# Output projection inside the expert stage's program, with a fine-grained start of head 0, in a one-core decoder-layer kernel

## The reference

```python
merged = sigmoid(parts[14]) * branch_a + sigmoid(parts[15]) * branch_b
x = x + ga1 * _rmsnorm(merged @ w_out, g_post1)          # output projection
h2 = _rmsnorm(x, g_pre2) * (1 + sc2) + sh2
# _peer(h2): per token, 8 heads
q = (h2 @ wq).reshape(T, 8, 256)
v1, i1 = top_k(q[..., :128] @ k1.T, 16)
v2, i2 = top_k(q[..., 128:] @ k2.T, 16)
sc, pos = top_k(all 256 sums v1 + v2, 16)                # 16 experts of 16384
g = softmax(sc)
act = gelu(einsum('td,thkd->thk', h2, u[eidx]))
f = einsum('thk,thkd->td', g * act, v[eidx])
x = x + ga2 * _rmsnorm(f, g_post2)
```

## Time and profile before

| | us |
|---|---|
| median of 3 runs (2635.83 to 2647.21) | 2636.57 |
| the profiled execution | 2642.91 |
| its span in the trace | 2641.1 |
| PE busy | 2226.0 (84%) |
| DVE busy | 1233.0 (47%) |
| ACT busy | 698.1 (26%) |
| POOL busy | 730.0 (28%) |
| gathers of the expert stage, issues on POOL | 576 |
| value matmuls (L1718) busy | 1084.4 |
| POOL idle ahead of a gather, for the value matmuls | 761.4 |
| DVE idle ahead of a dot product, for a gather | 428.4 |

### The profile page before, as it was taken

How to read it: one execution, slowest core, us unless ns; L and a number is a source line. 1 busy time by engine, 2 the same in 40 slices (tenths; PEclk the granted TensorE clock), 3 DMA queues, 4 the chain that set the end, 5 groups by cost and what they waited for, 6 DMA issues and landing times.

```text
span 2641.1 us, 24928 instructions
## 1 busy us (share of the span) xinstructions
PE 2226.0 (84%) x8970; PEld 1258.3 (48%) x8970; DVE 1233.0 (47%) x3186; ACT 698.1 (26%) x2115; POOL 730.0 (28%) x694
## 2 busy tenths in 40 slices
PE   6999989997787999878888887979788777787786
PEld 2777447865575776344443443434344333333221
DVE  1000001225232011457767667676776776767764
ACT  2000012332120001223333333333333443333322
POOL 0000001110101000034444443535444444454441
PEclk8999989997676999989999998989899898898899
DMA  7566648978672125079999999999999999999997
GB/s 279 228 252 253 249 142 303 318 307 333 222 270 104 60 72 179 4 281 420 416 418 417 413 419 409 420 406 420 410 418 412 415 421 404 420 415 414 418 418 301
DMA packets 134914, 850.41 MB, mean 322 GB/s; under 512 B 15121, under 2 KB 32817, under 8 KB 52989
## 3 DMA queue, kind: packets, MB, share of 16 engines
q0 software_dynamic: 85760, 691.32, 64.5%
q1 hardware_dynamic: 47740, 154.95, 15.9%
q10 hardware_dynamic: 1290, 2.55, 0.3%
HBM read 836.43 MB, written 99.37 MB: 354 GB/s over the span
## 4 chain that ended last, share of the span: by engine, by line
DMA 18%; PE 18%; DVE 17%; issue 2%; ACT 2%; POOL 1%; ACTq 0%; POOLq 0%
DMA pr_ring<-in_uv,pr_idx 18%; PE ps L1718 17%; DVE pr_ring L1859 4%; POOL pr_ring L1670 1%; DVE pr_hot L1843 1%; DVE pr_hot L1839 1%; DVE pr_ind L1820 1%; DVE pr_ind L1817 1%; DVE pr_pick L1846 1%; PE ps L1684 1%; ACT pr_coef L1777 1%; DVE pr_val L1819 1%; DVE pr_rest L1818 1%; DVE pr_val L1816 1%; DVE pr_pos L1820 1%
## 5 line engine op out<-in xcount | busy, mean ns | idle before, releaser
L1718 PE MATMUL ps<-pr_ring,pr_diag 128*128 128x512 f32 (+1 forms) x2304 | 1084.4, 626 | 288.9 <-ACT pr_diag L1781 288.5
L1670 POOL DMA_INDIRECT pr_ring<-in_uv,pr_idx x576 | 658.3, 1143 | 1129.1 <-PE ps L1718 761.4
L1859 DVE CUSTOM_DVE_ANT_0 pr_ring<-pr_ring,h 128x1024 f32<-128x1024 f32 x576 | 691.5, 1225 | 435.3 <-DMA pr_ring<-in_uv,pr_idx 428.4
L1718 PEld LDWEIGHTS ps<-pr_ring,pr_diag 128*128 128x128 f32 (+1 forms) x2304 | 438.4, 195 | 896.0 <-issue 510.2
L1772 ACT ACTIVATE pr_gel<-pr_dots 128x2 f32<-128x2 f32 x288 | 58.3, 202 | 637.5 <-DVE pr_dots L1859 637.3
L1781 ACT ACTIVATE pr_diag<-ident,pr_coef 128x128 f32<-128x128 f32 x512 | 173.5, 386 | 0.0
L1777 ACT ACTIVATE pr_coef<-pr_gel,pr_wgt 128x1 f32<-128x1 f32 x576 | 138.6, 287 | 27.6 <-ACT pr_gel L1772 1.1
L1415 PE MATMUL ps<-trunk,mg_ring 128*128 128x288 f32 x512 | 129.2, 412 | 12.6 <-DMA mg_ring<-in_w_merge 12.6
L1684 PE MATMUL ps<-trunk,pr_wq 128*128 128x192 f32 (+1 forms) x512 | 132.1, 412 | 2.3 <-PEq L1480 1.3
L430 PE MATMUL ps<-trunk,ap_ring 128*128 128x288 f32 x384 | 126.3, 411 | 2.9 <-PEq L323 2.9
L431 PE MATMUL ps<-trunk,ap_ring 128*128 128x288 f32 x384 | 125.2, 408 | 0.0
(11 more groups left out here) (289 smaller groups left out, 2036.4 us busy)
## 6 DMA issues: line engine op xcount, KB each, us to landing
out_win_s<-in_cache POOLq DMA_DIRECT2D x64, 1020.0 KB, 7.9
sa_ring<-in_cache SPq DMA_DIRECT2D x24, 1024.0 KB, 7.7
late_ring<-in_w_ada SPq DMA_DIRECT2D x8, 2048.0 KB, 17.6
sa_ring<-in_kcacheB SPq DMA_DIRECT2D x16, 1024.0 KB, 7.6
out_win_s<-in_cache POOLq DMA_DIRECT2D x16, 1008.0 KB, 10.7
ap_ring<-in_w_attn_qk SPq DMA_DIRECT2D x6, 2048.0 KB, 11.4
mg_ring<-in_w_merge SPq DMA_DIRECT2D x16, 768.0 KB, 4.2
sa_ring<-in_kcacheA SPq DMA_DIRECT2D x8, 1280.0 KB, 5.9
```

Of the source, the lines that this page charges most:

```text
L1670: pool.indirect_dma_start(ring[:, n % RING, :], None, d["uv"], bass.IndirectOffsetOnAxis(ap=idx[:, b % 4, j:j + 1], axis=0)).then_inc(arri ...
L1718: mm = pe.matmul(ps[0:r, bank + half, :], diag[:, n % RING, 0:r], ring[:, n % RING, o:o + CHUNK], start=h == 0 and j == 0, stop=b == FINAL ...
L1859: ins = dve.tensor_tensor_reduce(u, u, e.h2[:, BLOCKS[b][0], :], 1.0, 0.0, ALU.mult, ALU.add, dots[:, n % RING:n % RING + 1])
```

## The change

- **One program for the output projection and the experts** (`output_and_experts`). The gather ring (10 slots) is allocated first; w_out, `merged` and the sample tile's modulation rows lie in its slots 2 to 9, the prompt's rows where gate2 and fy come later. ACT's squares write into `h2` instead of a scratch tile. mg_ring moves into `h2`, which has room for AHEAD = 3 units.
- **Head 0's queries** come in six pieces instead of four: tile 0 (128 columns) twice, tiles 1 and 2 (256) twice, tiles 3 and 4 (192) twice. The first four have PSUM banks of their own.
- **Order.** PE: product(0), product(1), turn(0), product(2), two query pieces, turn(1), scores(0), product(3), turn(2), product(4), turn(3), two pieces, turn(4), scores(1), two pieces, the loop. DVE: tiles 0 to 2, route(0), tiles 3 and 4, the loop. ACT in the order of its list in the diff.
- **Gathers.** The first two follow route(0); the third waits for all products (`s_mm`), the ninth for all of h2 (`s_h2`), the eleventh as before for the first row's matmuls.
- **route(1)** stands after the third batch (FIRST_ROUTE = 3).
- **Constants.** c_tri, c_stri and mh_norm_g are loaded in conv_and_gates, ahead of the cache pieces, on a semaphore of their own; mLSTM's DVE no longer waits for C0 and n0 at its first chunk.

```diff
@@ conv_and_gates, SP
+                for dst, src in ((m.tri[:], "c_tri"), (m.stri[:], "c_stri"), (m.mhg[:], "mh_norm_g")):
+                    sp.dma_start(dst, d[src]).then_inc(m.s_const, 16)
                 sa.load(sp, range(sa.SR))
@@ mlstm, SP and DVE
-                sp.dma_start(tri[:], d["c_tri"]).then_inc(s_in, 16)
-                sp.dma_start(stri[:], d["c_stri"]).then_inc(s_in, 16)
-                sp.dma_start(mhg[:], d["mh_norm_g"]).then_inc(s_in, 16)
                 sp.dma_start(C0[:], d["C0"]).then_inc(s_in, 16)
                 sp.dma_start(n0[:], d["n0"]).then_inc(s_in, 16)
...
                 sa.normalised(dve, chain)
-                dve.wait_ge(s_in, 80)
+                dve.wait_ge(m.s_const, 48)
                 for c in range(NCH):
@@ merge
-    AHEAD, UNITS = 4, 2 * KD
+    AHEAD, UNITS = 3, 2 * KD
-        ring = sb("mg_ring", [P, AHEAD, KD + H, P])
+        unit = (KD + H) * P
+        ring = e.h2[:].rearrange("p t n -> p (t n)")[:, 0:AHEAD * unit].rearrange("p (a c n) -> p a c n", a=AHEAD, n=P)
@@ head 0's pieces
+HEAD0 = 6
+def query_count(h, piece):
+    return piece if h == 0 else HEAD0 + 4 * (h - 1) + piece
+def query_span(h, piece):
+    spans = ((0, P), (P, GROUPED), (GROUPED, T)) if h == 0 else ((0, GROUPED), (GROUPED, T))
+    return slice(*spans[piece // 2]), piece % 2
+def query_bank(h, piece):
+    return (4, 5, 2, 3)[piece] if h == 0 and piece < 4 else QUERY_BANK
-ROUTE, SCORE, SCORED = 6, 2, 4
+FIRST_ROUTE, ROUTE, SCORE, SCORED = 3, 6, 2, 4
@@ output_and_experts, SP
                 sp.dma_start(keysT[:], d["keysT"]).then_inc(s_keys, 16)
+                sp.wait_ge(s_h2, NCH)
                 sp.dma_start(e.h2[TS:P, PT, :], e.h2[0:TS, PT, :]).then_inc(s_in, 16)
...
                 for h in range(QUERY_SLOTS, PH):
-                    sp.wait_ge(s_q, 4 * (h - QUERY_SLOTS + 1))
+                    sp.wait_ge(s_q, query_count(h - QUERY_SLOTS + 1, 0))
@@ POOL
                         n = b * TOPK + j
+                        if n == 2:
+                            pool.wait_ge(s_mm, NCH)
+                        if n == 8:
+                            pool.wait_ge(s_h2, NCH)
                         if n >= RING:
                             pool.wait_ge(s_v, n - RING + 1)
@@ PE, ahead of the loop
+                product(0)
+                product(1)
+                turn(0)
+                product(2)
+                pe.wait_ge(s_tt, 1)
                 query(0, 0)
                 query(0, 1)
+                turn(1)
+                pe.wait_ge(s_y1, 3)
                 pe.wait_ge(s_keys, 16)
                 scores(0)
-                scores(1)
+                product(3)
+                turn(2)
+                product(PT)
+                turn(3)
+                pe.wait_ge(s_y1, 4)
+                pe.wait_ge(s_tt, 3)
                 query(0, 2)
                 query(0, 3)
+                turn(PT)
+                pe.wait_ge(s_y1, NCH)
+                scores(1)
+                pe.wait_ge(s_tt, NCH)
+                query(0, 4)
+                query(0, 5)
+                pe.wait_ge(s_qt, 4)
@@ ACT, ahead of the loop
+                product_root(0)
+                trunk_root(0)
+                turned(0)
+                product_root(1)
+                trunk_root(1)
+                product_root(2)
                 query_taken(0, 0)
                 query_taken(0, 1)
+                turned(1)
                 scores_taken(0)
-                scores_taken(1)
+                trunk_root(2)
+                route_exp(0)
+                turned(2)
+                product_root(3)
+                trunk_root(3)
+                product_root(PT)
+                turned(3)
                 query_taken(0, 2)
                 query_taken(0, 3)
-                route_exp(0)
+                trunk_root(PT)
+                turned(PT)
+                scores_taken(1)
+                query_taken(0, 4)
+                query_taken(0, 5)
@@ DVE
+                dve.wait_ge(front.s_x, 32)
+                dve.wait_ge(front.s_r, 16 * 3 * (1 + NS))
+                for i in range(GROUP):
+                    input_of(i)
                 route(0)
-                dve.wait_ge(s_in, 16 * (2 + NS))
+                for i in range(GROUP, NCH):
+                    input_of(i)
                 for b in range(len(BLOCKS)):
                     for q in range(PER):
-                        if b == 0 and q == 1:
+                        if b == 0 and q == FIRST_ROUTE:
                             route(1)
@@ build
-            output_projection(nc, k, d, e, o)
-        peer(nc, k, d, e)
+        e.ring, e.gf = sb("pr_ring", [P, RING, 2 * D]), sb("pr_gf", [P, 3, D])
+        o.w = flat[:, at:at + 2 * KD * CHUNK].rearrange("p (n c x) -> p n c x", n=2, c=KD)
...
+        merge(nc, k, d, e, o)
+        output_and_experts(nc, k, d, e, o)
```

More of the change, by code:

```diff
@@ L1584, with output_and_experts @@
 PER = TOPK // BATCH
-ROUTE, SCORE, SCORED = 6, 2, 4
+FIRST_ROUTE, ROUTE, SCORE, SCORED = 3, 6, 2, 4
 SQUARE, MEAN, ROOT, FINISH = 2, 3, 4, 5
-def peer(nc, k, d, e):
+def output_and_experts(nc, k, d, e, front):
     with ExitStack() as ctx:
         sb = lambda n, s, dt=F32: ctx.enter_context(nc.sbuf_tensor(n, s, dt))
-        ring = sb("pr_ring", [P, RING, 2 * D])
+        ring, gate2, fy = e.ring, e.gf[:, 0:2], e.gf[:, 2]
+        ss = sb("op_ss", [P, 2, NCH, 2])
+        ms = sb("op_ms", [P, 2, NCH])
+        rt = sb("op_rt", [P, 2, NCH])
+        rs = sb("op_rs", [P, 2, NCH])
+        s_mm, s_sq, s_ms, s_rt, s_y1, s_x1, s_h2, s_tr, s_tt = (
+            k.sem("op_" + n) for n in ("mm", "square", "ms", "root", "taken", "x1", "h2", "turned", "turned_taken"))
         keysT = sb("pr_keysT", [P, 2, NKEYS])
@@ L1676, in query @@
                 def query(h, piece):
-                    group, half = divmod(piece, 2)
-                    cols = slice(GROUPED, T) if group else slice(0, GROUPED)
+                    cols, half = query_span(h, piece)
                     if piece == 0:
                         pe.wait_ge(e.wq_ready[h % QUERY_SLOTS], 16 * (h // QUERY_SLOTS + 1))
-                    pe.wait_ge(s_qt, 4 * h + piece)
+                    if h > 0 or piece >= 4:
+                        pe.wait_ge(s_qt, query_count(h, piece))
                     for c in range(KD):
-                        mm = pe.matmul(ps[:, QUERY_BANK, 0:cols.stop - cols.start],
+                        mm = pe.matmul(ps[:, query_bank(h, piece), 0:cols.stop - cols.start],
                                        e.wq[:, h % QUERY_SLOTS, c, half * P:(half + 1) * P], e.h2T[:, c, cols],
@@ L1691, in scores @@
                     r = tile_rows(i)
-                    pe.wait_ge(s_qt, 4 * h + (2 if i < GROUP else 4))
+                    pe.wait_ge(s_qt, 2 if b == 0 else query_count(h, 4 if h == 0 else 2) if i < GROUP else query_count(h + 1, 0))
                     if b >= 1:
@@ L1731, in query_taken @@
                 def query_taken(h, piece):
-                    group, half = divmod(piece, 2)
-                    f = 2 * h + half
-                    act.wait_ge(s_q, 4 * h + piece + 1)
-                    if group == 0:
-                        ins = act.activation(first[:, f % 4, :], ps[:, QUERY_BANK, 0:GROUPED], ACT.Copy)
-                    else:
-                        ins = act.activation(e.later[:, f, :], ps[:, QUERY_BANK, 0:T - GROUPED], ACT.Copy)
-                    ins.then_inc(s_qt, 1)
+                    cols, half = query_span(h, piece)
+                    f, n = 2 * h + half, cols.stop - cols.start
+                    act.wait_ge(s_q, query_count(h, piece) + 1)
+                    dst = first[:, f % 4, cols] if cols.start < GROUPED else e.later[:, f, :]
+                    act.activation(dst, ps[:, query_bank(h, piece), 0:n], ACT.Copy).then_inc(s_qt, 1)
                 def scores_taken(b):
@@ L1782, in diags, with product_root @@
                                        scale=coef[:, o + j:o + j + 1]).then_inc(s_dg, 1)
+                def product_root(i):
+                    r = tile_rows(i)
+                    act.wait_ge(s_mm, i + 1)
+                    for n in range(2):
+                        chain.step(act.activation(e.h2[0:r, i, 0:CHUNK], ps[0:r, 2 * (i % 2) + n, :], ACT.Square,
+                                                  accum_out=ss[0:r, 0, i, n:n + 1]))
+                    act.sem_inc(s_sq, 1)
+                    act.wait_ge(s_ms, 2 * i + 1)
+                    act.activation(rt[0:r, 0, i:i + 1], ms[0:r, 0, i:i + 1], ACT.Sqrt).then_inc(s_rt, 1)
@@ new lines, in trunk_root, with turned @@
+                def trunk_root(i):
+                    r = tile_rows(i)
+                    act.wait_ge(s_x1, i + 1)
+                    act.activation(e.h2[0:r, i, :], e.x1[0:r, i, :], ACT.Square,
+                                   accum_out=ss[0:r, 1, i, 0:1]).then_inc(s_sq, 1)
+                    act.wait_ge(s_ms, 2 * i + 2)
```

(20 more changed lines are left out.)

167 lines of the change are left out of this document (59 added, 108 removed).

## The result

| | before | after |
|---|---|---|
| median of 4 runs each, us | 2641.89 (2635.83 to 2650.15) | 2612.12 (2593.49 to 2621.62) |
| the profiled execution | 2642.91 | 2621.62 |
| its span in the trace | 2641.1 | 2619.8 |

The ratio is 0.9869, with an interval of 0.9832 to 0.9906: 34.6 us faster (25 to 44), where 36.6 was forecast. The medians in the table lie 29.8 us apart; the ratio on record is not that of the medians, and its interval holds both. 2600 was under both medians and the range 2587 to 2614 holds the first.

What follows compares the result with a forecast made beforehand. The expert stage was taken as bound by a full DMA pipe of 576 gathers of 1 MB. Terms of 27.5 + 4.2 + 4.9 = 36.6 us off the median 2636.57 gave 2600 us, range 2587 to 2614.

Steps and rivals of the forecast that it cites:

- Term 1: Expert stage: ten rows fetched early and an earlier pipe restart, less a hole, save 27.5 us (22 to 32).
- all at full clock: Early bound for the first value matmul: 1136 us, with 128-column query pieces at 1.8 us, against 1139.3 forecast.
- the hole: Start of the value loop: 3 us of idle DMA pipe, between 0 and 6, as query(1,0) delays the thirteenth gather.
- three slots: Rival: the merge with three slots makes PE wait at each of 16 units, 2650 us; chance 0.03.
- the early rows bring nothing: Rival: route(0) on DVE delays the projection, value matmuls start as late as before, 2627 us; chance 0.04.
- the prologue's tail is longer: Rival: ACT's order and half clock put the first value matmul at 1145, hole 6 us, total 2609; chance 0.12.
- Term 2: Start of mLSTM: DVE's first chunk no longer waits for n0 behind C0, 4.2 us saved.
- Costs: Three issues moved ahead in the convolution stage, 0 to 1.3 us, taken as 0; merge with three units also 0.
- Term 3: mLSTM's first sums on PE keep the upper clock once the idle gap goes: 4.9 us saved, bounds 0 and 7.
- lower clock: Rival: terms 1 and 2 hold but mLSTM's sums stay at 1.2 GHz, 2605 us; chance 0.20.

Runs made afterwards that it cites:

- experts alone: The change with the three constants loaded back in mLSTM's program and its waits as before, so the merged expert program only: 2621.73 us, ratio 0.9916.
- store early: The change with conv_and_gates' store of m_new issued ahead of the later cache loads instead of behind them: 2606.51 us, ratio 0.9854.
- constants alone: The kernel before with only the three constants loaded early in the convolution stage: 2638.70 us, ratio 0.9995.
- the change again: The changed kernel, unaltered, run again beside later experiments: 2619.88 us, ratio 0.9882.
- filled waits: The change with four thrown-away matmuls (the fill) ahead of two parts of sampled-attention products, where PE waits for cache pieces: 2604.61 us, ratio 0.9849.
- late rows: The change with the first gather held until head 0's last query piece is copied, so no row is fetched under the projection: 2626.94 us, ratio 0.9944.
- filled stage end: All four with the sums kept, plus three thrown-away matmuls of 512 columns at the end of conv_and_gates: 2594.97 us, ratio 0.9807.
- query later: The change with head 1's first query piece after the third batch of rows instead of after the first: 2609.67 us, ratio 0.9885.
- root first: The change with ACT taking trunk_root of tile 4 ahead of the copy of query piece (0,3): 2603.95 us, ratio 0.9851.
- constants behind: Filled stage end with the three constant loads issued behind the first cache loads and the mask instead of ahead: 2596.67 us, ratio 0.9815.
- all four with the sums kept: The change with store early, filled waits, query later and root first, the added matmuls not starting a sum: 2599.46 us, ratio 0.9819.

## Why the prediction was right, point by point

**Term 1, the early rows, right to 1 us.** 26.6 us against 27.5. Of its steps: first gather +62.2 (forecast +64.2), the six at +76.0 (+77.7), the last two at +88.5 (+91), first value matmul at +101.1 (+104), the eleventh gather 3.8 us behind that (2.2). The narrow query pieces were the over-priced step: 128 columns twice took 3.73 us together where 2.6 each was taken, so the "all at full clock" bound was the right end for them. The thirteenth gather came 6.9 us behind the twelfth, behind query(1,0) of 5.32 us, and the hole was 2.5 us (3). Beyond its first 20 us the value loop showed no share under 0.95 in any stretch of 20 us (in 5 us stretches, some of 0.90). The experts alone, store early and after agree within 0.3 us (C 1579.2, 1579.0, 1579.2). Where product(0) took 15.67 us on both sides, the term is 27.5 (constants alone against the change again) or 28.9 (against filled waits). In the sum's own cut, the eleventh gather is issued 6.1 us ahead of where the first one was (+104.9 against +111.0; forecast 4.8), and from there to the end it takes 20.4 us less (1474.4 against 1494.8; forecast 25.7 - 3 = 22.7). With the hole of 2.5 us the ten rows gave 22.9 us and not the 25.7 of ten times 2.57. Where the other 2.8 went stays open, so part of the agreement is two misses that offset each other. The late rows split the term another way, 13.7 to 15.0 us for the early rows and 13.9 for the shorter way.

**The free things were free.** PE waited for the merge's ring once, for 12.6 us at its start, in both kernels; SP issued its last query weight at 1029.91 for 7.20 us, 3 us ahead of product(0). The rival "three slots" did not occur, nor did "the early rows bring nothing"; the first value matmul at +101.1 excludes "the prologue's tail is longer".

**Term 2, right where it was made and given back where it was taken as free.** DVE's first chunk came 7.02 us behind mLSTM's start in ten of the twelve traces without the wait (4.97 and 4.49 in the two with the filled stage end). With the wait it was 11.17 in before and 10.1 in the experts alone, so the gain is 3.6 to the mean of the two, 4.15 to before. The failed step is "Costs", three issues "between 0 and 1.3, I take 0". A is 96.2 us in the mean of the two traces with the constants in mLSTM, and 99.4 in the seven with them early and the store late (96.8 to 101.7): 3.2 us. From the stage's first load to DVE's first chunk that leaves 106.8 against 106.4 (103.9 to 108.7), 0.4 us in the mean. Of these, 2.5 lie ahead of DVE's masks (89.6 against 92.1 in twelve traces) and the rest in the store of m_new. The masks' delay begins at the row transposes of the gates (L992 in the experts alone, L994 in after), here in these two:

```profile
639.68 5.25 PE L992 MATMUL ps<-ident,m_rows 4*128 4x4 f32 x40
644.86 1.88 PE L995 MATMUL ps<-m_decay,sel 4*128 4x12 f32 x8
```
```profile
640.72 7.93 PE L994 MATMUL ps<-ident,m_rows 4*128 4x4 f32 x40
648.58 1.88 PE L997 MATMUL ps<-m_decay,sel 4*128 4x12 f32 x8
```

They begin 57.7 us into the stage instead of 56.4 (means of twelve and two): 1.3 us. And they take 7.2 us instead of 6.0 in the mean, since 8 of the 12 ran wholly at 1.2 GHz (7.92 or 7.93) and neither of the two did: 1.2 us. The first cache load was issued 2.7 us into the stage without constants ahead of it and 4.1 with them, but the fourth at 15.0 and 16.1 us without, 15.3 to 16.2 in the twelve, so the issues themselves show no clear cost. Why the transposes start later, and whether their clock follows from the change at all with two traces on one side, stays open. The run of the constants alone (1.3 us) agrees with so small a net, but its interval would allow the full 4.2 too.

**Term 3, a toss.** The sums of chunk 0 were at 5.5 to 5.9 us in 5 of the 12 traces without the wait (rows late, store early, query later, root first, constants behind), and at 10.4 in the other seven, after's among them; in neither of the two with the wait. None of two against five of twelve does not show that it was the wait that kept the clock down. If it was, the term is worth 5/12 of 4.9, 2.0 us, and not 4.9. The failed step is "with no idle time between, the sums most likely keep the clock that had been granted": in after 690 to 692 has PE busy 2.00 of 2.00 us and a clock of 0.50, where before had it idle and at 1.00. The rival "lower clock" is what the profiled execution shows, and 0.20 was too small a chance for it. The Trainium skill (TensorE: Matmul & The Clock Gate, Part 1) had said that the point of change varies from run to run; these traces agree, with 5 and 7.

**The sum again.** 26.6 + (3.6 - 3.2) + 2.0 = 29.0 us against 34.6 (25 to 44) and 31.2 (22 to 40) measured: inside both. The mechanism of term 1 was right; that the whole came within 2.0 us of 36.6 is partly luck, since terms 2 and 3 gave 2.4 us and not 9.1. Of the 12.1 us between 2600 and after's median, 5.3 are in the level of before, which the three runs shown gave as 2636.57 and later sets as 2641.89, 2641.07 (23 runs), 2639.64, 2645.24 and 2643.13. The other 6.8 are the change, whose medians are 29.8 and not 36.6 us apart: terms 2 and 3.

**What spreads the runs.** B is 120.7 us with all four chunks' sums at the upper clock, 130.6 to 132.7 with three, 134.0 to 135.0 with two, 139.7 to 144.7 with one, 149.2 and 150.1 with none: some 7 us a chunk in the mean, the size given to them in the prediction. (Two of the groups counted as upper changed level on the way and took 6.2 and 6.3 us.) The kernels without the fill spread from 130.6 to 150.1 for the same work, two thirds of the effect studied; the change alone had 144.7 and 150.1 in its two traces. Without the fill, 8 of 27 later chunks' sums (chunks 1 to 3 of nine traces) were at the upper clock; with it, 15 of 15.

**The better version.** "Filled stage end" (2594.97; runs 2588.59 to 2599.91) beats both kernels: 1.9% under before and, on the same chip, 24.9 us under the change (2619.88; 2596.74 to 2629.36; the lowest of these is under the highest of the other). "Constants behind" (2596.67) can't be told from it. The two traces of that chip are 29.8 us apart: 19.3 in B (all four chunks' sums at the lower clock against one of them), 3.9 in C, 2.4 in A, 2.1 from mLSTM's start to its first sums, and 1.8 ahead of A. The gains in C do not add up: root first gave 3.3 us, query later 2.2 to 3.6, and the four kernels with both have C 1577.3 to 1578.0, 2.5 to 4.6 less than the change again and filled waits.

## What to carry to other kernels

Where one stage is bound by a full DMA pipe, every transfer that can be landed ahead of it is worth nearly its whole time on the pipe, and the forecast can be made by counting them, less the idle time that follows while the ring refills: ten rows of 2.57 us are 25.7 us, and 20.4 were gained behind a hole of 2.5. An engine's strict order decides where such a prologue waits: one step moved ahead of one copy on ACT gave 3.3 us. A gain at the head of a program is only that if the program's start stays put, so look at what the last DMA of the program ahead does; and where short matmuls alternate with waits, first read the granted clock over several traces, because its two levels can move more than the edit. Even a length cut out around the edit, such as C, has to be checked for it: product(0) at its start moved C by 1.7 us and had hidden most of what query later gained.

## What the runs showed of the hardware

- The clock can fall without any idle time. In store early PE was busy 16.00 of 16.00 us, on the sums, products of the sampled attention and the next chunk's scores, when it fell from 1.00 to 0.50 (PE alone):

```profile
690.00:698.00 8.00, 8.00 (x144) 1.00 0.01 2
698.00:702.00 4.00, 4.00 (x80) 1.00 0.63 214
702.00:704.00 2.00, 2.00 (x10) 0.78 1.04 398
704.00:706.00 2.00, 2.00 (x27) 0.50 1.05 389
```

  Rows late shows the same at 702 to 706, all four with the sums kept at 732 to 736. And in after PE was busy 10.00 of the 10.00 us from 640 to 650, on short matmuls of 4 and 12 columns, and the clock stayed at 0.50, where it had been since 626. I had taken an unbroken row of work as what holds the clock. With the fill in the later waits it stayed at 1.00 for the sums of chunks 1 to 3 in five traces of five (5.52 us each).
- The Trainium skill (PSUM — Partial Sum Buffer, The four PSUM rules) says that a matmul with its first flag clears the accumulation marks of the whole bank, not only those of the columns it writes. The fill agrees: with `start=True` into unused columns, the sample tokens' sums in the same bank came out altered; with `start=False` they did not. The two profiled executions, on two chips, took 2604.94 and 2602.80 us.
- A store of one small tile, issued behind the last cache loads, held the program boundary: the next program began 7.7 us after its issue in after (675.66 to 683.36) and 5.6 to 7.6 us in the other eight traces with the store there; once it was issued some 50 us earlier, the next program began 5.1 us behind the masks, in five traces of five.
